# Prompt attention of a two-layer hybrid decoder: the query blocks of a head in the order 0, 7, 1, 6, 2, 5, 3, 4

## The chip, the cores and the metric

The kernel runs on one core of one Trainium2 chip. The metric is the device time of one execution in microseconds. The times are those of whole executions; a profile is of one execution and shows its span from the first to the last instruction.

## What is computed

One inference step of two consecutive layers for a prompt of 1024 tokens and a decode batch of 8 sequences with 4 new tokens each. A layer has an input projection, an mLSTM group of heads and a latent attention (MLA) group of heads, an output projection, a convolutional FFN and a per-layer input embedding. The change lies in the prompt's part of the latent attention, which the reference sweeps in blocks of 128 queries, each against the keys up to its own end:

```python
    def one_block(i):
        q = lax.dynamic_slice_in_dim(qcat, i * qb, qb, axis=1)
        s = jnp.einsum('bqhd,bkd->bhqk', q, lat).astype(jnp.float32) * scale
        qpos = i * qb + jnp.arange(qb)
        s = jnp.where(kpos[None, :] <= qpos[:, None], s, -jnp.inf)
        p = jax.nn.softmax(s, axis=-1).astype(vals.dtype)
        return jnp.einsum('bhqk,bkr->bqhr', p, vals)
    o = lax.map(one_block, jnp.arange(nb))
```

The kernel computes it with keys and values expanded per head, 4 heads of 128 + 64 query columns and 128 value columns, in float32. Block i of a head has i + 1 key tiles of 128, so block 7 is eight times as long as block 0. The blocks don't depend on each other.

## The kernel before, in words

The program loops over the two layers (L2201). In each it projects the input (`mix_projection`), prepares queries, keys and values (`mla_prepare`), runs the prompt's attention (`mla_prompt`, L1356), the decode batch's attention (`mla_sample`, L1485), the output projection, the FFN and the embedding. Each of these is a phase of its own: it ends in a barrier over all engines (L142), so no work of the next phase begins before the last instruction of this one.

`mla_prompt` has a list `blocks` of 32 pairs (head h, query block i), which sets the order of the work on every engine. Each engine's instructions are written out by hand against the place n in this list; buffers go by n modulo 2 (scores: two PSUM banks each; probabilities and their transposes in SBUF: two of each; output: a PSUM bank each), and the groups of up to four transposes go through two PSUM banks by a running number q. Columns of queries, keys and output go by h and i.

- TensorE: scores of block 0; then in step n the scores of block n+1 (L1389 for the 128 plain columns, L1390 for the 64 rotated ones, one pair for each 512 keys), the value products of block n-1 (L1400, one matmul for each key tile), a wait for `p_made` of block n, and its transposes (L1416, one for each key tile). In the trace a float32 matmul of L1389, L1390 or L1400 is two records and a transpose one, so x12 at L1400 is six key tiles.
- VectorE, per block: adds the causal mask (L1453), takes the row maximum (L1458), turns it into the bias of the exponential (L1460); after the exponential the reciprocal of the row sum (L1473) and the scaling of the probabilities (L1475). In step n it does the reciprocal and the scaling of block n, then mask, maximum and bias of block n+1, then the copy of the output of block n-2 (L1466).
- ScalarE: the exponential of block n (L1438), then the copies of the transposes of block n-1 from PSUM (L1429), one for each group of up to four key tiles.
- SyncE issues the loads of 32 pages of the decode batch's cache (L1354), which the next phase reads, and waits for them at the end.

The order inside a step stands here:

```python
            for n in range(len(blocks)):
                if n + 1 < len(blocks):
                    scores(n + 1)
                if n:
                    values(n - 1)
                pe.wait_ge(ph["p_made"], n + 1)
```

`values(n)` waits for `pt_made` up to the last group of block n and for the output bank; `scores(n)` waits for the exponential of block n-2, whose banks it writes.

Of the kernel before, what the change touches and what calls it, by code (L numbers as in the profile page):

```python
# [33 lines left out]
A_HEADS, A_NOPE, A_ROPE, A_DV = 4, 128, 64, 128  # L34
# [1321 lines left out]
def mla_prompt(nc, core, kr, qn, qr, kn, vt, cat, pages):  # L1356


    with ExitStack() as st:
# [6 lines left out]
            exp_done=1, rec_step=1, p_made=1, tr_done=1, pt_made=1, o_done=1, o_used=1, pages_loaded=1))  # L1366
        ps = core.psum
        QT = SEQ // P
        blocks = [(h, i) for h in range(A_HEADS) for i in range(QT)]
        groups = [[(n, j0, min(j0 + 4, i + 1)) for j0 in range(0, i + 1, 4)] for n, (h, i) in enumerate(blocks)]  # L1370
        first_group = np.cumsum([0] + [len(g) for g in groups]).tolist()

# [805 lines left out]
def build_program(nc, operands, n_pool):  # L2178
# [4 lines left out]
    with ExitStack() as whole:  # L2183
# [17 lines left out]
        with nc.Fori(0, DEPTH) as l:  # L2201
            core.l = l
            load_phase(nc, [(core.vec[:], core.vec_in[ds1(l)].rearrange("l p n -> (l p) n"))])
            mem = MixTensors(core.slab)
            mix_projection(nc, core, mem)
            mla_prepare(nc, core, mem)
            pages = [core.slab.at(M_PAGES + i * PW, f"pages_{i}", [P, PW]) for i in range(4)]
            mla_prompt(nc, core, mem.kr, mem.qn, mem.qr, mem.kn, mem.vt, mem.cat, pages)
            mla_sample(nc, core, mem.ckv, mem.kr, mem.qn, mem.qr, mem.cat, pages)
            X = core.slab.at(X_AT, "x", [P, KX, NT])  # L2210
            out_projection(nc, core, mem.cat, X)
            conv_ffn(nc, core, X)
            layer_embedding(nc, core, X)
# [160 lines left out]
```

## Time and profile before

| | us |
|---|---|
| runs, median (lowest to highest) of 3 | 3465.0 (3461.5 to 3472.26) |
| the profiled execution | 3464.91 |
| its span | 3463.1 |
| prompt attention, layer 0 (443.2 to 585.2) | 142.0 |
| prompt attention, layer 1 (2149.8 to 2288.6) | 138.8 |

The mean granted clock of TensorE over the span is 0.944 of full speed. TensorE is busy for 90% of the span, VectorE for 45%, ScalarE for 31% and GpSimd for 4%. In the rows PE is TensorE, DVE is VectorE, ACT is ScalarE. A row of the timeline has the start in us from the span's start, the length in us, the engine, the line of the kernel, the operation, what is written and read, the shapes and how many instructions were merged; in brackets stands how long the engine had been idle before it, and what ended that.

### The profile page before, as it was taken

How to read it: one execution, taken by the hardware profiler on the slowest of the kernel's cores; microseconds unless marked ns; L12 is line 12 of the kernel's file. 1: busy time of each engine (PE TensorE's matmuls, PEld its weight loads, DVE VectorE, ACT ScalarE, POOL GpSimd, SP SyncE). 2: the span in 40 equal slices, each digit the busy share in tenths (PEclk: the TensorE clock that was granted, in tenths of full speed). 3: DMA queues.
4: the chain of work that ended last, by engine and by line, in shares of the span. 5: the costliest groups of instructions: out<-in, count | busy, mean ns of one | idle time of the engine just before them, and what ended most of it. 6: DMA issues, size and time to landing. Idle time of an engine off the chain costs nothing. (4 is left out here: it accounts for less than half of the span.)

```text
span 3463.1 us, 49081 instructions
## 1 busy us (share of the span) xinstructions
PE 3104.8 (90%) x19219; PEld 2881.7 (83%) x19219; DVE 1541.2 (45%) x2460; ACT 1064.0 (31%) x1994; POOL 144.5 (4%) x248
## 2 busy tenths in 40 slices
PE   5998898498999999997979988966899999999887
PEld 5997754298999999997979976535899999999887
DVE  4233543235554445447351354522454445445563
ACT  4232322214223332334242223322233332333241
POOL 0000300000000000000000021000000000000000
PEclk9998899699999999998989989987999999999998
DMA  5102131402111111102131021223111111111023
GB/s 206 47 25 80 45 110 40 167 15 78 49 38 49 37 50 49 50 13 85 42 123 37 19 78 68 83 82 139 41 49 50 37 50 49 39 48 44 10 92 132
DMA packets 58324, 220.52 MB, mean 64 GB/s; under 512 B 6635, under 2 KB 22507, under 8 KB 42995
## 3 DMA queue, kind: packets, MB, share of 16 engines
q1 hardware_dynamic: 58098, 217.27, 17.5%
q8 instruction: 172, 2.82, 0.3%
q14 instruction: 54, 0.43, 0.0%
HBM read 189.72 MB, written 27.52 MB: 63 GB/s over the span
## 5 line engine op out<-in xcount | busy, mean ns | idle before, releaser
L209 PE MATMUL psum<-h_high,conv_ffn_weight_parts 128*128 128x352 f32 x2112 | 689.9, 327 | 21.8 <-DVE h_low L314 14.3
L211 PE MATMUL psum<-h_high,conv_ffn_weight_parts 128*128 128x352 f32 x2112 | 686.3, 325 | 0.0
L210 PE MATMUL psum<-h_low,conv_ffn_weight_parts 128*128 128x352 f32 x2112 | 682.3, 323 | 0.0
L1909 DVE SCALAR_TENSOR_TENSOR conv_sum<-u_padded,vectors,conv_sum 128x1024 f32<-128x1024 f32 x176 | 226.1, 1285 | 594.3 <-ACT conv_sum L1858 581.8
L209 PEld LDWEIGHTS psum<-h_high,conv_ffn_weight_parts 128*128 128x128 f32 x2112 | 400.5, 190 | 24.9 <-issue 23.4
L210 PEld LDWEIGHTS psum<-h_low,conv_ffn_weight_parts 128*128 128x128 f32 x2112 | 399.0, 189 | 0.0
L211 PEld LDWEIGHTS psum<-h_high,conv_ffn_weight_parts 128*128 128x128 f32 x2112 | 396.8, 188 | 0.0
L209 PE MATMUL psum<-g_parts,conv_ffn_weight_parts 128*128 128x352 f32 x1056 | 345.8, 327 | 27.2 <-DVE g_parts L1920 16.3
L211 PE MATMUL psum<-g_parts,conv_ffn_weight_parts 128*128 128x352 f32 x1056 | 343.5, 325 | 0.0
L210 PE MATMUL psum<-g_parts,conv_ffn_weight_parts 128*128 128x352 f32 x1056 | 343.3, 325 | 0.0
L1928 DVE TENSOR_TENSOR x<-x,psum 128x352 f32<-128x352 f32 x528 | 255.5, 517 | 119.4 <-PE psum L211 118.5
L1854 ACT ACTIVATE u_padded<-psum 128x352 f32<-128x352 f32 (+1 forms) x264 | 120.4, 456 | 540.1 <-PE psum L211 540.1
L209 PEld LDWEIGHTS psum<-g_parts,conv_ffn_weight_parts 128*128 128x128 f32 x1056 | 200.3, 190 | 33.5 <-issue 16.8
L209 PE MATMUL psum<-h_high,_projection_weight_parts 128*128 128x352 f32 x576 | 191.9, 333 | 14.3 <-DVE h_low L314 14.3
L210 PEld LDWEIGHTS psum<-g_parts,conv_ffn_weight_parts 128*128 128x128 f32 x1056 | 200.2, 190 | 0.0
L211 PEld LDWEIGHTS psum<-g_parts,conv_ffn_weight_parts 128*128 128x128 f32 x1056 | 199.4, 189 | 0.0
L1867 ACT ACTIVATE g_parts<-conv_sum 128x1056 fp32r<-128x1056 f32 x44 | 47.8, 1087 | 486.9 <-PE psum L211 404.5
L211 PE MATMUL psum<-h_high,_projection_weight_parts 128*128 128x352 f32 x576 | 187.3, 325 | 0.0
L210 PE MATMUL psum<-h_low,_projection_weight_parts 128*128 128x352 f32 x576 | 186.9, 324 | 0.0
L1858 ACT ACTIVATE conv_sum<-psum,vectors 128x352 f32<-128x352 f32 x264 | 170.7, 647 | 0.0
L203 DVE TENSOR_TENSOR conv_ffn_weight_parts<-conv_ffn_weight_stage,conv_ffn_weight_parts 128x2048 fp32r<-128x2048 f32 x66 | 151.1, 2290 | 23.9 <-ACT conv_ffn_weight_parts L197 23.9
L209 PE MATMUL psum<-heads_high,_projection_weight_parts 128*128 128x352 f32 x384 | 126.5, 330 | 23.4 <-DVE heads_low L1706 23.4
(332 smaller groups left out, 5454.3 us busy)
## 6 DMA issues: line engine op xcount, KB each, us to landing
conv_ffn_weight_stage<-w_up_dram SPq DMA_DIRECT2D x44, 1024.0 KB, 5.0
conv_ffn_weight_stage<-w_down_dram SPq DMA_DIRECT2D x22, 1024.0 KB, 4.8
_projection_weight_stage<-w_in_dram SPq DMA_DIRECT2D x18, 1024.0 KB, 4.8
pages<-cache_dram SPq DMA_DIRECT2D x64, 288.0 KB, 4.3
mix_work<-x_residual SPq DMA_DIRECT2D x16, 528.0 KB, 3.8
x<-x_residual SPq DMA_DIRECT2D x2, 4224.0 KB, 16.5
x_residual<-x SPq DMA_DIRECT2D x16, 528.0 KB, 2.7
_projection_weight_stage<-w_out_dram SPq DMA_DIRECT2D x8, 1024.0 KB, 5.9
```

The lines of the kernel that those rows point to most:

```text
L203: dve.tensor_tensor(dst[:, 1, 0:width], self.stage[:, slot % self.stages, 0:width], dst[:, 0, 0:width].bitcast(F32), ALU.subtract).then_in ...
L209: pe.matmul(out, lhs[0], rhs[0], start=first, stop=False)
L210: pe.matmul(out, lhs[0], rhs[1], start=False, stop=False)
L211: return pe.matmul(out, lhs[1], rhs[0], start=False, stop=last)
L1854: act.activation(u[:, q, 2 + c * CH:2 + c * CH + n], src[:, 0:n], ACT.Copy)
L1858: op = act.activation(t[:, q, chunk(c)], src, ACT.Identity, bias=bias, scale=w2)
L1867: act.activation(gp[:, 0, slot, :], t[:, 1, :], ACT.Copy).then_inc(ph["ghi_made"], 1)
L1909: dve.scalar_tensor_tensor(t[:, q, 0:SEQ], row[:, tap:tap + SEQ], w, t[:, q, 0:SEQ], ALU.mult, ALU.add).then_inc(ph["conv_step"], 1)
L1928: dve.tensor_tensor(X[:, k, chunk(c)], X[:, k, chunk(c)], ps[:, (6 + n) % 8, 0:CH], ALU.add).then_inc(ph["x_made"], 1)
```

## The change

The order of the blocks within a head becomes 0, 7, 1, 6, 2, 5, 3, 4 in place of 0 to 7. Nothing else is changed: the list still has the 32 pairs, head by head.

```diff
--- before.py
+++ after.py
@@ -1366,7 +1366,8 @@
             exp_done=1, rec_step=1, p_made=1, tr_done=1, pt_made=1, o_done=1, o_used=1, pages_loaded=1))
         ps = core.psum
         QT = SEQ // P
-        blocks = [(h, i) for h in range(A_HEADS) for i in range(QT)]
+        order = [i for pair in zip(range(QT // 2), range(QT - 1, QT // 2 - 1, -1)) for i in pair]
+        blocks = [(h, i) for h in range(A_HEADS) for i in order]
         groups = [[(n, j0, min(j0 + 4, i + 1)) for j0 in range(0, i + 1, 4)] for n, (h, i) in enumerate(blocks)]
         first_group = np.cumsum([0] + [len(g) for g in groups]).tolist()
```

## Rows read from the trace of the kernel before

**Rows 1.** The page, part 1: busy time, share of the span, instructions.

```profile
PE 3104.8 (90%) x19219; PEld 2881.7 (83%) x19219; DVE 1541.2 (45%) x2460; ACT 1064.0 (31%) x1994; POOL 144.5 (4%) x248
```

**Rows 2.** Stretches: the stage in layers 0 and 1, then two inside it.

```profile
core 0: us, PE busy (x) PEld busy (x) DVE busy (x) ACT busy (x) POOL busy (x), PEclk, DMA share, GB/s
443.20:585.20 142.00, 135.98 (x624) 78.97 (x624) 66.83 (x192) 46.96 (x113) 0.00 (x0) 0.95 0.20 67
2149.80:2288.60 138.80, 132.74 (x624) 77.59 (x624) 66.81 (x192) 46.96 (x113) 0.00 (x0) 0.98 0.21 69
444.70:458.30 13.60, 13.46 (x26) 5.95 (x26) 5.65 (x20) 3.30 (x11) 0.00 (x0) 0.50 0.52 174
2151.40:2158.10 6.70, 6.52 (x13) 2.79 (x13) 3.15 (x13) 2.14 (x8) 0.00 (x0) 0.50 0.34 101
```

**Rows 3.** TensorE's waits, stage of layer 0: us in total, times, longest.

```profile
PE psum L1400 <- ACT probs_T L1429: 5.5, 5, 1.6
```

**Rows 4.** Timeline, layer 0, block 7 of a head, its seam, the next seam.

```profile
508.82 1.60 PE L1400 MATMUL psum<-probs_T,a_v 128*128 128x128 f32 x12
...
510.26 0.93 PE L1416 MATMUL psum<-constants,probs 128*128 128x128 f32 x7
...
511.02 0.39 PE L1389 MATMUL psum<-a_k,a_q_nope 128*128 128x128 f32 x2
...
511.81 0.97 ACT L1429 ACTIVATE probs_T<-psum 128x512 f32<-128x512 f32 x2
...
512.14 0.75 DVE L1475 TENSOR_SCALAR probs<-probs,softmax_rows 128x1024 f32<-128x1024 f32 x1
...
512.83 1.83 PE L1400 MATMUL psum<-probs_T,a_v 128*128 128x128 f32 x14 [1.01 <-ACT probs_T L1429]
...
514.50 1.04 PE L1416 MATMUL psum<-constants,probs 128*128 128x128 f32 x8
...
546.07 1.83 PE L1400 MATMUL psum<-probs_T,a_v 128*128 128x128 f32 x14 [1.01 <-ACT probs_T L1429]
```

**Rows 5.** Timeline, layer 0, the first short blocks of the next head.

```profile
515.37 0.60 PE L1389 MATMUL psum<-a_k,a_q_nope 128*128 128x256 f32 x2
...
516.52 2.05 PE L1400 MATMUL psum<-probs_T,a_v 128*128 128x128 f32 x16
...
518.41 0.27 PE L1416 MATMUL psum<-constants,probs 128*128 128x128 f32 x1
...
518.52 0.81 PE L1389 MATMUL psum<-a_k,a_q_nope 128*128 128x384 f32 x2
518.78 0.28 ACT L1429 ACTIVATE probs_T<-psum 128x128 f32<-128x128 f32 x1 [0.61 <-PE psum L1416]
...
520.10 0.49 PE L1400 MATMUL psum<-probs_T,a_v 128*128 128x128 f32 x2
...
520.43 0.38 PE L1416 MATMUL psum<-constants,probs 128*128 128x128 f32 x2
```

**Rows 6.** Timeline, layer 0, block 4 of that head.

```profile
526.37 0.94 PE L1400 MATMUL psum<-probs_T,a_v 128*128 128x128 f32 x6
...
528.64 0.59 ACT L1429 ACTIVATE probs_T<-psum 128x512 f32<-128x512 f32 x1
...
528.97 0.55 DVE L1475 TENSOR_SCALAR probs<-probs,softmax_rows 128x640 f32<-128x640 f32 x1
```

**Rows 7.** Timeline, layer 0, the end of the stage.

```profile
579.31 1.83 PE L1400 MATMUL psum<-probs_T,a_v 128*128 128x128 f32 x14 [1.65 <-ACT probs_T L1429]
...
580.97 1.04 PE L1416 MATMUL psum<-constants,probs 128*128 128x128 f32 x8
...
582.81 2.05 PE L1400 MATMUL psum<-probs_T,a_v 128*128 128x128 f32 x16 [0.80 <-ACT probs_T L1429]
```

**Rows 8.** Timeline, layer 0, the start of the stage.

```profile
443.28 0.46 PE L1389 MATMUL psum<-a_k,a_q_nope 128*128 128x128 f32 x2 [1.72 <-PEq L142]
...
444.08 0.70 PE L1389 MATMUL psum<-a_k,a_q_nope 128*128 128x256 f32 x2
```

## The prediction

> **What bounds the kernel now.** I read the busy shares first, then the busy time and granted clock of the stretches in which the prompt attention runs, then TensorE's waits there, then its timeline through one head. TensorE is busy for 90% of the span [rows 1]. The change touches one stage, which runs once per layer, for 142.0 and 138.8 us; in it TensorE is busy 96% of the time, VectorE under half, ScalarE a third [rows 2]. So what counts is the time in which TensorE stands still. The waits view finds 5.5 us per layer, all of it in front of the value products, on ScalarE's copies of the transposed probabilities [rows 3].
>
> Call S(i), V(i) and T(i) the scores, value products and transposes of the block with i+1 key tiles. TensorE's order in step n is S of block n+1, V of block n-1, a wait for block n's probabilities, T of block n. While block n goes through mask, maximum, exponential, reciprocal and scaling on VectorE and ScalarE, TensorE has V(n-2), T(n-1), S(n+1) and V(n-1) to do: that is its cover. The timeline gives both. Matmul ends are modelled and overlap, so I take lengths of PE work between starts. V(7) runs 516.52 to 518.41, 1.89 us, and V(0) 520.10 to 520.43, 0.33: 0.11 + 0.222 per key tile. T(7) is 0.87 and T(0) 0.11: 0.109 per tile. S(1) is 1.15 and S(2) 1.58 [rows 4, 5]. S(0) is 0.80, at a point where the clock was still full [rows 8].
>
> The chain of block 7, counted from the end of its scores (V(5) starts at 508.82): the copies behind its exponential start at 511.81, after 2.99 us; the scaling ends at 512.14 + 0.75 = 512.89, and with 0.05 us from the end to TensorE's start (as between the copies' end at 512.78 and V(6) at 512.83) the transposes can go after 4.12 us [rows 4]. The chain of block 4, from 526.37: the copy of the block before it (0.59) ends at 529.23, so V can go after 2.91 us; scaled at 529.52, so T after 3.20 [rows 6]. Blocks 5 and 6 lie between, at about 3.5 and 3.8 (estimates between those two).
>
> As a check, the seam of before: V(6) is ready 4.01 us after the end of S(7), TensorE gets there after V(5) 1.44, T(6) 0.76, S(0) 0.80 = 3.00, so it should wait 1.01 us, and the row has 1.01 [rows 4]. In rising order every other block finds a cover as long as its chain, as the cover grows with it.
>
> **The change, term by term.** It removes and adds no instruction: the S, V and T of a head are the same and sum to the same TensorE time. It only changes who covers whom. No DMA is moved: the 32 page loads of this stage are issued by SyncE without a wait on a block. The terms, per layer:
>
> 1. Removed: the seam 7 to 0 between heads, 3 x 1.01 = 3.03 us. Removed at the end: V(6) without a next S in its cover waits 4.01 - 2.20 = 1.81, and the last T(7) to V(7) takes 1.84 for 0.87 of transposes, 0.97 idle [rows 7]. Sum 5.81. (The waits view shows somewhat less for the last two, since it counts from modelled ends.) The very first T also waits a little for block 0, which I take as 0.14: between 0 and, at most, a short chain of 2 us less S(1), 1.15.
>
> 2. Added, block 7 beside two short ones: cover V(4) 1.22 + T(0) 0.11 + S(1) 1.15 + V(0) 0.33 = 2.81 against 4.12. Wait 1.31 us, in two pieces. V(0) comes first, in TensorE's queue, and its copy stands behind exp(7) on ScalarE: ready at 2.99 + 0.28 + 0.05 = 3.32, reached at 2.48, so 0.84; then T(7) 0.47 more. Queued behind these waits is all of TensorE's work, so they are on the path. 3 heads x 1.31 = 3.93.
>
> 3. Added, the same in the first head, which has no V(4) before it: 4.12 - 1.59 = 2.53.
>
> 4. Added, block 4 beside 3 and the next head's 0: V(3) is reached at V(5) 1.44 + T(3) 0.44 + S(0) 0.80 = 2.68 and ready at 2.91: 0.23, three times 0.69.
>
> 5. The end on block 4: V(3) is reached at 1.88, ready at 2.91: 1.03. The last T(4) to V(4) saves 0.31 of the second copy (0.28 for 0.59): 1.84 - 0.31 - 0.55 = 0.98. Sum 2.01.
>
> 6. At nothing: block 6 (cover V(7) 1.89 + T(1) 0.22 + S(2) 1.58 + V(1) 0.55 = 4.24 against 3.8), block 5 (V(6), T(2), V(2) and more than S(2): over 4.3 against 3.5), blocks 1, 2, 3 and the next 0, whose chains start when VectorE is free of the long one and are over under the following long scores (7, 6, 5 and 8 tiles of keys, where S(2) with 3 takes 1.58). If that cover went, a short chain of about 2 us would show. The leads of 0.4 us for block 6 are the thinnest.
>
> Per layer 9.16 - 5.95 = +3.2 us, so +6.4 for two; the head's period goes from 33.24 (V(6) at 512.83 to V(6) at 546.07 [rows 4]) to 33.8.
>
> 7. The clock at the start. The granted clock stands at half, the 1.2 GHz level, for 13.6 us in layer 0 from 444.7 on and for 6.7 us in layer 1 [rows 2], while TensorE works nearly all the time, so half of each is lost: 3.35 us in layer 1, and 3.2 more in layer 0, by which the two stages differ. In the new order S(7) comes second; it is about 4.1 us of work (an estimate: 0.43 more per tile than S(2) up to four tiles, 2.01, and twice that). At half clock it fills those first 7 us, so layer 1 loses the same 3.35. In layer 0 S(7) would end at about 451.7 (3.5 us of it done at half clock), block 7's chain runs to 455.8, where a slow TensorE costs nothing because it waits anyway (its cover of 1.59 takes 3.2), and only the 2.5 us to 458.3 cost again: 3.5 + 1.25 = 4.8 lost in place of 6.55, a gain of 1.7. So +6.4 - 1.7 = +4.7. Bounds on this term: -3.2 (layer 0 needs no second stretch at half clock and nothing comes instead) to +6.4 (the 2.53 us of idleness in the first head brings one more stretch in each layer, each 3.2).
>
> The profiled execution took 3464.9 us for a span of 3463.1, 0.1 from the median of 3465.0. Forecast: 3464.9 + 4.7 = 3469.6 us, +0.14%. A measurement of this kernel can tell about 0.3%, 10.4 us, from no change, so this is no change, with a lean to the slow side.
>
> **Rivals.** (a) Slower, by the clock: every seam now has 1.31 us of waits in two pieces within 2 us, and TensorE's clock goes to half behind each. For it: at the start of the stage the clock fell after a pause of 1.7 us in front of S(0) [rows 2, 8]. Against: it stayed full across the 1.01 us seams, and across 1.81 and 0.97 us near the end of the stage, for the granted clock of the whole stage is 0.95 and 0.98, which the two stretches at its start account for alone (6.8 of 142.0, 3.35 of 138.8) [rows 2, 7]. Price: 3.2 us for each fall, at 8 seams 25.6, 3495 us. It decides from two falls on (4.7 + 6.4 = 11.1 against the bound of 10.4). Chance 0.17.
> The Trainium skill, TensorE: Matmul & The Clock Gate, "A second HAM failure mode: psum-queue depth-cycling", says that short idle times between groups of matmuls that cycle through PSUM banks can make the clock swing between its levels. By that rule this change comes out at rival (a); the trace so far speaks against it.
>
> (b) Faster, the pairing works as a cover: if V(0) did not have to stand behind exp(7) and the long chain were covered, terms 2 to 4 vanish and 3464.9 - 2 x (5.95 - 2.01) = 3457.0. For it: per pair, cover and chain balance in sum. Against: the queues are in order and the cover of block 7 is counted from rows. Chance 0.03 (and 0.02 for the clock's best bound with a good measurement).
>
> (c) The change doing nothing: the expression gives 0, 7, 1, 6, 2, 5, 3, 4, and all buffers go by the place n, all columns by i, so the order does change. That leaves 3465 only as a sum that cancels, inside the forecast's case.
>
> **How the numbers follow.** Forecast's case 0.78, within 0.3%: 3465 to 3476 by the bounds of term 7 and 0.15 us of error in each of some ten waits. Rival (a) with a few falls only reaches 3480. Range 3464 to 3479. Same 0.78; slower 0.17; faster 0.05.
>
> **What would show it.** In the waits view, idle time in front of V on ScalarE's copies rises from 5.5 us per layer to about 7, and T shows waits on VectorE's scaling that it hardly has now, about 0.47 each at four places, 1.9; together near 9. From one head's block 7 mask to the next 33.8 us. The stage in layer 1 takes 142 us. The step on the clock is wrong if a stretch at half clock stands anywhere but at the stage's start; the whole reading is wrong if the waits on block 7 are absent, or if S, V or T change in length.

## The result and the profile after

The changed kernel takes 3476.9 us (median of 20 runs, 3469.2 to 3485.8) against 3469.8 (20 runs, 3461.5 to 3483.7) for the kernel before. The ratio is 1.0018 with a 95% interval of 1.0010 to 1.0025: 6.2 us slower, 3.5 to 8.7 (the two medians lie 7.1 us apart). That is inside the 0.3% that the prediction called no change, and on its slow side; a ratio of 1 lies outside the interval. The forecast was 3469.6, +4.7 us. Its base, 3464.9, came from three runs; over 20 runs the kernel before takes 4.9 us more than that, so the measured 3476.9 stands 7.3 us above the forecast, most of it by the base, and it is the difference that tests the working.

The busy time and granted clock of the stage in both layers of the changed kernel, the answer to [rows 2]; the last number but two is the granted clock:

```profile
core 0: us, PE busy (x) PEld busy (x) DVE busy (x) ACT busy (x) POOL busy (x), PEclk, DMA share, GB/s
444.10:587.60 143.50, 136.65 (x624) 78.72 (x624) 66.53 (x192) 46.71 (x113) 0.00 (x0) 0.95 0.20 67
2150.80:2294.30 143.50, 136.64 (x624) 78.71 (x624) 66.54 (x192) 46.70 (x113) 0.00 (x0) 0.95 0.20 67
445.80:459.30 13.50, 12.64 (x24) 5.20 (x23) 4.38 (x13) 3.48 (x9) 0.00 (x0) 0.50 0.52 176
2152.50:2166.00 13.50, 12.64 (x24) 5.20 (x23) 4.38 (x13) 3.48 (x9) 0.00 (x0) 0.50 0.55 176
```

The stage takes 143.5 us in either layer, where it took 142.0 and 138.8: +1.5 and +4.7. Layer 1 now has the same 13.6 us at half clock as layer 0. (The windows in these rows lie just inside the stretch; read to its ends it is 13.65 us, written 13.6 or 13.7 here, and the short one is 6.8.) The span is 3467.4 us, 4.3 longer: 6.2 from the two stages, and 2 us less elsewhere, where nothing was changed.

TensorE's waits in the stage of layer 0 (us in total, times, longest), the answer to [rows 3]. Line numbers are one higher than before:

```profile
PE psum L1401 <- ACT probs_T L1430: 5.5, 9, 0.9
...
PE psum L1417 <- DVE probs L1476: 1.0, 3, 0.3
```

The same 5.5 us on ScalarE's copies, in nine waits in place of five, and 1.0 us on VectorE's scaling that was not there. The seam at block 7, from the timeline of layer 0, the answer to [rows 4]; the last row is V(4) one head later:

```profile
487.50 1.38 PE L1401 MATMUL psum<-probs_T,a_v 128*128 128x128 f32 x10
...
488.72 0.27 PE L1417 MATMUL psum<-constants,probs 128*128 128x128 f32 x1
488.83 0.60 PE L1390 MATMUL psum<-a_k,a_q_nope 128*128 128x256 f32 x2
...
490.49 0.27 ACT L1430 ACTIVATE probs_T<-psum 128x128 f32<-128x128 f32 x1
...
490.81 0.49 PE L1401 MATMUL psum<-probs_T,a_v 128*128 128x128 f32 x2 [0.76 <-ACT probs_T L1430]
490.83 0.75 DVE L1476 TENSOR_SCALAR probs<-probs,softmax_rows 128x1024 f32<-128x1024 f32 x1
...
491.63 1.09 PE L1417 MATMUL psum<-constants,probs 128*128 128x128 f32 x8 [0.33 <-DVE probs L1476]
...
492.56 1.02 PE L1390 MATMUL psum<-a_k,a_q_nope 128*128 128x512 f32 x2
...
521.35 1.38 PE L1401 MATMUL psum<-probs_T,a_v 128*128 128x128 f32 x10
```

From the end of S(7), 487.50: V(0) starts after 3.31 us, behind its copy, which stands behind the long exponential; T(7) after 4.13. Forecast were 3.32 and 4.12. A head takes 521.35 - 487.50 = 33.85 us; 33.8 was forecast, 33.24 it was.

### The profile page after: what moved, and what is told of

It reads as the page before. It is cut to its first block and busy times, and to the rows that moved or that the text cites. A ratio compares the mean times of both kernels' runs of the same rounds, so it can differ in the third digit from the quotient of the medians.

```text
span 3467.4 us, 49081 instructions
## 1 busy us (share of the span) xinstructions
PE 3111.6 (90%) x19219; PEld 2884.7 (83%) x19219; DVE 1541.2 (44%) x2460; ACT 1063.6 (31%) x1994; POOL 144.5 (4%) x248
## 5 line engine op out<-in xcount | busy, mean ns | idle before, releaser
L209 PEld LDWEIGHTS psum<-g_parts,conv_ffn_weight_parts 128*128 128x128 f32 x1056 | 199.8, 189 | 33.6 <-issue 16.8
L203 DVE TENSOR_TENSOR conv_ffn_weight_parts<-conv_ffn_weight_stage,conv_ffn_weight_parts 128x2048 fp32r<-128x2048 f32 x66 | 151.2, 2290 | 23.9 <-ACT conv_ffn_weight_parts L197 23.9
```

The lines of the kernel that those rows point to most:

```text
L203: dve.tensor_tensor(dst[:, 1, 0:width], self.stage[:, slot % self.stages, 0:width], dst[:, 0, 0:width].bitcast(F32), ALU.subtract).then_in ...
L209: pe.matmul(out, lhs[0], rhs[0], start=first, stop=False)
```

## Experiments

In all of them the result is set against runs of the kernel before on the same chip. The stage's time is read from the profile; the stretch at half clock at its start is read from its ends (granted clock 0.50) and can be checked by the stage's mean clock: 0.97 or 0.98 is 6.8 us, 0.96 is 10.2, 0.95 is 13.6, 0.94 is 17.1, as long as the clock is full from there to the end of the stage.

### Neighbours of like length

```diff
-        order = [i for pair in zip(range(QT // 2), range(QT - 1, QT // 2 - 1, -1)) for i in pair]
+        order = [0, 2, 4, 6, 7, 5, 3, 1]
```

> Order 0, 2, 4, 6, 7, 5, 3, 1 in every head: each block stands between neighbours of nearly its own length, also across the heads. My theory (the cover of a block's softmax chain is V of two blocks before, T of the block before, S of the next, V of the block before, all counted from rows): block 7 has V(4) 1.22 + T(6) 0.76 + S(5) 3.26 + V(6) 1.66 = 6.9 us of cover against 4.12, and no block of a head waits; what is left is about 0.8 us at the end of the stage. TensorE's waits fall from 5.5 us per layer to about 1, a head takes 32.25 us (33.24 before, 33.85 after the change), and the time falls by 5.1 us per layer, 10 us in all: ratio 0.997 to the kernel before. Rival (mixing lengths costs in itself, since TensorE's order and the two buffers are made for neighbours that grow by one): waits of 0.2 to 1 us stay at the steps of two, ratio 1.000 or above.

Ratio 0.9984 (0.9975 to 0.9992), 3465.6 us against 3472.5. The waits of the stage in layer 0:

```profile
PE psum L1390 <- PEq L142: 1.7, 1, 1.7
PE psum L1401 <- ACT probs_T L1430: 1.3, 2, 0.7
```

and the row of T(7) of its first head in the timeline:

```profile
465.63 0.75 DVE L1476 TENSOR_SCALAR probs<-probs,softmax_rows 128x1024 f32<-128x1024 f32 x1
...
467.55 1.83 PE L1401 MATMUL psum<-probs_T,a_v 128*128 128x128 f32 x14
469.21 1.04 PE L1417 MATMUL psum<-constants,probs 128*128 128x128 f32 x8
```

The scaling of block 7 ends at 466.38, TensorE asks for it at 469.21. (The first row of the waits is the barrier at the stage's start, alike in all kernels.) A head takes 32.34 us, 32.25 and the 0.11 us at V(3). So the covers counted from rows hold, and mixing lengths costs nothing where the cover is there. At the end of the stage 1.3 us were left, where I expected 0.8. The stage takes 136.3 us in both layers, 10.2 of them at half clock at the start. That is 7.2 us less per layer than the changed order. In the whole time I expected 10 us, and 5.6 were measured (2.8 to 8.7): by the two stages it is 8.2 against the profile of before shown above and 5.3 against the second one below.

### The mirror image

```diff
-        order = [i for pair in zip(range(QT // 2), range(QT - 1, QT // 2 - 1, -1)) for i in pair]
+        order = [1, 3, 5, 7, 6, 4, 2, 0]
```

> Order 1, 3, 5, 7, 6, 4, 2, 0 in every head, the mirror image of the pyramid. Theory (covers from rows): the 0.11 us that the pyramid waits at V(3), whose cover had only S(0), goes, since the block with S(0) as its next one, 2, has V(6) 1.66 + T(4) 0.55 + S(0) 0.81 = 3.02 us before V(4), ready at 2.7. No wait inside the stage but at its end, about 0.8 us; a head takes 32.25 us. Stage 136.0 us, less whatever the clock at the start does; ratio to before 0.998. Rival: the steps of two leave their own waits, 0.1 to 0.3 us per head as in the pyramid.

Ratio 0.9980 (0.9969 to 0.9992). A wait of 0.17 us stood before V(4) in every head, so the 2.7 us that I gave for its copies were too short, and a head took 32.40 us, not 32.25. The rival was right in this. The stages:

```profile
446.20:584.30 138.10, 136.06 (x624) 78.66 (x624) 67.16 (x192) 47.60 (x113) 0.00 (x0) 0.95 0.21 69
2153.00:2288.00 135.00, 132.88 (x624) 77.12 (x624) 67.18 (x192) 47.61 (x113) 0.00 (x0) 0.97 0.22 71
```

138.1 us in layer 0 and 135.0 in layer 1, with 13.7 and 6.8 us at half clock: the same program, 3.1 us apart by one more stretch, as in the kernel before.

### The pairs read backwards

```diff
-        order = [i for pair in zip(range(QT // 2), range(QT - 1, QT // 2 - 1, -1)) for i in pair]
+        order = [3, 4, 2, 5, 1, 6, 0, 7]
```

> Order 3, 4, 2, 5, 1, 6, 0, 7, the changed order read backwards, so the same pairs. Theory: what counts are the four pieces of cover, not who is whose partner. Block 7 now has V(6) 1.66 + T(0) 0.11 + S(3) 2.01 + V(0) 0.33 = 4.11 against 4.12, so no wait; block 6 has V(5) 1.44 + T(1) 0.22 + S(0) 0.81 + V(1) 0.55 = 3.02 against 3.83, so 0.8 us; block 5 has V(2) ready at 3.05 and reached at 2.70, so 0.35 us. A head takes 33.4 us (33.85 in the changed kernel). At the end of the stage 3.0 us. Rival (block 7 beside block 0 is the cost): waits of 1.3 us stay at block 7 and a head takes 33.85 us.

One execution, 3483.1 us. Waits of 0.28 us at V(2) and 0.72 at V(1) in each head (0.81 in the first; 0.35 and 0.8 were expected), none at block 7 except behind the last one; a head takes 33.53 us. So block 7 beside block 0 costs nothing with S(3) and V(6) around it: the pairing is not the cost, the four pieces of cover are. The stage's waits in layer 0:

```profile
PE psum L1401 <- ACT probs_T L1430: 6.2, 10, 1.4
...
PE psum L1417 <- DVE probs L1476: 0.3, 1, 0.3
```

The stage is nonetheless long, 146.1 and 145.7 us. At its end block 7 has only V(6) and T(0) as cover, and TensorE waits three times within 4.1 us; the end in layer 0, and the granted clock of two stretches there:

```profile
584.70 0.49 PE L1401 MATMUL psum<-probs_T,a_v 128*128 128x128 f32 x2 [1.37 <-ACT probs_T L1430]
585.52 1.09 PE L1417 MATMUL psum<-constants,probs 128*128 128x128 f32 x8 [0.33 <-DVE probs L1476]
587.41 3.78 PE L1401 MATMUL psum<-probs_T,a_v 128*128 128x128 f32 x16 [0.80 <-ACT probs_T L1430]
...
583.00:586.70 3.70, 1.91 (x13) 1.25 (x12) 1.73 (x7) 1.80 (x4) 0.00 (x0) 1.00 0.00 0
586.80:591.50 4.70, 3.78 (x16) 3.49 (x16) 0.26 (x1) 0.56 (x2) 0.00 (x0) 0.50 0.00 0
```

The clock fell to half at 586.7, inside the third of these waits, 4.8 us before the stage ended, and V(7) took 3.78 us in place of 2.05. In layer 1 it was the same, 4.4 us before the end. No other kernel showed that.

### ScalarE's copy ahead of the long exponential

```diff
+                early = n > 0 and blocks[n - 1][1] == 0
+                if early:
+                    transposed(n - 1)
                 act.activation(pr[:, b, 0:(i + 1) * P],
...
-                if n:
+                if n and not early:
                     transposed(n - 1)
```

> The changed order, but ScalarE copies the transposes of block 0 before the exponential of block 7, not behind it. My theory (the length of block 7's chain against its cover of 2.81 us sets the seam, and the copy's place only splits the wait): V(0) no longer waits, T(7) waits the whole 1.3 us, a head still takes 33.85 us, the time is that of the changed kernel, ratio 1.0018 to before. Rival (the copy that stands behind the long exponential is the cost): the 0.84 us at three seams and the 2.06 us in the first head go, 4.6 us per layer, ratio 0.9992 to before.

The seam of this kernel in the timeline of layer 0:

```profile
491.48 1.38 PE L1401 MATMUL psum<-probs_T,a_v 128*128 128x128 f32 x10
...
493.96 0.49 PE L1401 MATMUL psum<-probs_T,a_v 128*128 128x128 f32 x2
...
495.78 1.09 PE L1417 MATMUL psum<-constants,probs 128*128 128x128 f32 x8 [1.33 <-DVE probs L1479]
```

V(0) waits no more, and T(7) waits it all: it starts 4.30 us after S(7)'s end, 0.17 later than before, because the copy now holds up the exponential by as much. A head takes 34.01 us. So the copy's place splits the wait and doesn't make it; moving it costs a little. The time, though, went up more than that: ratio 1.0035 (1.0022 to 1.0048). The profile shows where:

```profile
448.00:591.80 143.80, 136.28 (x624) 78.70 (x624) 66.25 (x192) 46.64 (x113) 0.00 (x0) 0.95 0.20 67
2155.00:2305.20 150.20, 142.73 (x624) 82.00 (x624) 66.25 (x191) 46.88 (x113) 0.00 (x0) 0.91 0.19 64
2156.30:2180.10 23.80, 22.70 (x48) 10.36 (x47) 7.23 (x20) 4.58 (x11) 0.00 (x0) 0.50 0.64 207
2275.90:2279.10 3.20, 3.20 (x10) 1.76 (x8) 1.21 (x5) 1.65 (x4) 0.00 (x0) 0.50 0.02 5
```

In layer 1 the start stood at half clock for 23.8 us, and the clock fell once more, at 2275.8, 0.1 us after the wait of 1.33 us at the last head's T(7), for 3.4 us. That makes the two stages together 7.0 us longer than in the changed kernel, about what the ratio shows (1.0035 against 1.0018 is 5.9 us). All five executions took 3481.7 to 3486.8 us, but only this one has a profile. I took a second one:

> The kernel with block 0's copy ahead of the exponential of block 7 once more, for a second profile. Theory (one wait of 1.33 us in place of 0.84 and 0.49 is what the clock does not bear): again stretches at half clock behind some seam inside the stage, or a start of over 20 us at half clock, in at least one layer. Rival (chance): 13.6 us at the start in both layers and full clock from there, stages of 143.8 us.

This one took 3475.8 us and showed neither: 13.7 us at the start in both layers, full clock from there, stages of 143.8 us. So with one wait of 1.33 us the clock can fall at a seam, and it did at one of the 12 seams that were reached at full clock in two profiles. In the changed kernel, with 0.84 and 0.49 us (by starts), it fell at none of 12. One fall doesn't show that the joining of the waits is the cause, and why the first ratio was 1.0035 stays open beyond its one profile.

### The changed kernel again, and the kernel before again

> The changed kernel once more, for a second profile. Theory (the second stretch at half clock comes with block 7 standing second in the first head): 13.6 us at half clock at the start of the stage in both layers, stages of 143.5 us. Rival (chance): about 7 us in one or both, that stage 1.5 to 3 us shorter.

> The kernel before once more, for a second profile. A stage of 142.0 us where the start shows 13.6 us at half clock, of 138.8 us where it shows 6.8. If the rising order brings the shorter stretch in at least one of the two layers again, as in three of four so far, the first head's order has to do with it; if both show 13.6, the difference between the orders was chance.

The changed kernel: 143.5 and 143.6 us, 13.7 us at half clock in both layers. The kernel before:

```profile
444.40:583.40 139.00, 132.55 (x624) 77.43 (x624) 66.80 (x192) 46.95 (x113) 0.00 (x0) 0.98 0.21 69
2154.60:2293.50 138.90, 132.61 (x624) 77.44 (x624) 66.76 (x192) 46.97 (x113) 0.00 (x0) 0.98 0.21 69
446.50:453.10 6.60, 6.03 (x12) 2.46 (x11) 3.35 (x12) 1.87 (x8) 0.00 (x0) 0.50 0.39 115
2156.50:2163.10 6.60, 6.15 (x13) 2.47 (x11) 3.17 (x12) 2.08 (x8) 0.00 (x0) 0.50 0.40 113
```

6.8 us in both. The 13.6 us of layer 0 in [rows 2] was the rarer case of the kernel before, not what layer 0 is like.

### Only the first head, or only the others

```diff
-        blocks = [(h, i) for h in range(A_HEADS) for i in order]
+        blocks = [(h, i) for h in range(A_HEADS) for i in (order if h else range(QT))]
```

> The first head of each layer rises from 0 to 7, the other three go in the changed order. My theory by waits: 1.0 us at the seam 7 to 0, 0.64 us at the first block 7 that has V(7) in its cover, 1.31 at two seams, 0.23 at two, 2.0 at the end, 6.9 us per layer with the start, 0.9 above the kernel before: ratio 1.0005. On the clock, theory: the pause of 2.5 us in the first head brings the second stretch at half clock, so here at least one of the two layers shows only about 7 us at half clock at the start of the stage. Rival: that second stretch is chance, and both layers may show 13.6 us here too.

Ratio 1.0001 (0.9990 to 1.0012). Its stages:

```profile
448.40:588.30 139.90, 133.57 (x624) 77.60 (x624) 66.49 (x192) 46.55 (x113) 0.00 (x0) 0.98 0.21 68
2158.30:2298.30 140.00, 133.50 (x624) 77.53 (x624) 66.48 (x192) 46.57 (x113) 0.00 (x0) 0.98 0.21 68
```

6.8 us at half clock in both. The waits are as counted: 1.01 at the seam, 0.42 in two pieces at the first block 7 in the waits view, 0.76 + 0.33 at the later ones.

```diff
-        blocks = [(h, i) for h in range(A_HEADS) for i in order]
+        blocks = [(h, i) for h in range(A_HEADS) for i in (range(QT) if h else order)]
```

> Only the first head of each layer goes in the changed order, the other three rise. My theory by waits: 2.5 us in the first head, 0.2 at its end, 1.0 at each of the two seams 7 to 0, 2.8 at the end: 7.6 us per layer, 1.6 above the kernel before, 3.2 in all; with the second stretch at half clock in both layers some 1.5 to 3 us more: ratio 1.001 to 1.0018. Both layers show 13.6 us at half clock at the start of the stage. Rival (the three steady heads make the loss): ratio 1.0003 or less, and the stretch at half clock is 7 us in one of them as before.

Ratio 1.0013 (1.0004 to 1.0022). Its stages:

```profile
446.30:588.00 141.70, 135.77 (x624) 78.64 (x624) 66.83 (x192) 46.98 (x113) 0.00 (x0) 0.95 0.21 67
2156.90:2298.60 141.70, 135.76 (x624) 78.61 (x624) 66.83 (x192) 46.95 (x113) 0.00 (x0) 0.95 0.21 67
```

13.6 us at half clock in both. The changed order lost 4.6 us per layer against the usual 138.9 of the kernel before: its first head alone loses 2.8 (141.7), its other three heads alone 1.1 (139.9 and 140.0). The parts add up to 3.9 of 4.6; the seams that each of the two kernels has between the orders differ from both pure ones, and I did not take that apart.

### Block 7 second, but covered

```diff
-        order = [i for pair in zip(range(QT // 2), range(QT - 1, QT // 2 - 1, -1)) for i in pair]
+        order = [0, 7, 6, 5, 4, 3, 2, 1]
```

> Order 0, 7, 6, 5, 4, 3, 2, 1 in every head. Block 7 stands second as in the changed kernel, but its cover has S(6): in a later head V(1) 0.55 + T(0) 0.11 + S(6) 3.69 + V(0) 0.33 = 4.68 us against 4.12, in the first head 4.13. Theory on the waits: none inside a head, 32.3 us per head, waits only at the end of the stage. On the clock, theory A (the pause at block 7 of the first head brings the second stretch): here the stretch at the stage's start is 7 to 10 us in at least one layer. Theory B (it comes with the long scores that stand second, pause or not): 13.6 us in both layers, stages of about 138 us. Ratio to before 0.997 by A, 0.999 by B.

Ratio 0.9988 (0.9973 to 1.0003). No wait inside a head, 32.23 us each, and the stage still takes 139.2 us:

```profile
443.20:582.40 139.20, 137.65 (x624) 79.08 (x624) 66.93 (x192) 47.99 (x113) 0.00 (x0) 0.94 0.21 69
2149.80:2289.00 139.20, 137.65 (x624) 79.09 (x624) 66.90 (x192) 48.00 (x113) 0.00 (x0) 0.94 0.21 69
444.70:461.50 16.80, 16.80 (x28) 6.21 (x27) 4.84 (x12) 2.69 (x6) 0.00 (x0) 0.50 0.58 195
2151.30:2168.20 16.90, 16.90 (x28) 6.24 (x27) 4.85 (x12) 2.81 (x7) 0.00 (x0) 0.50 0.58 189
```

TensorE works without a pause for 16.8 us, and all of them at half clock. (The whole stretch at half clock is 17.1 us.) So theory A, that the pause at block 7 brings the second stretch, fell. Theory B, that it comes with the long scores that stand second, fits, but its numbers were too small: 13.6 us and a stage of about 138 us, against 17.1 and 139.2. That the long scores are the cause is not shown, and why is open. By first head, the stretch at half clock at the start of the stage was, over all profiles:

| order of the first head | kernels | us at half clock, layer 0 / layer 1 |
|---|---|---|
| 0, 1, 2, 3 ... | before, twice; first head rising; the last one below | 13.7/6.8, 6.8/6.8, 6.8/6.8, 6.8/13.7 |
| 0, 2, 4, 6 ... | pyramid | 10.2/10.2 |
| 1, 3, 5, 7 ... | its mirror | 13.7/6.8 |
| 3, 4, 2, 5 ... | pairs backwards | 13.7/13.7 |
| 0, 7, 1, 6 ... | changed, twice; first head paired; copy ahead, twice | 13.7/13.7 three times, 13.7/23.9, 13.7/13.7 |
| 0, 7, 6, 5 ... | this one | 17.1/17.1 |

Part of the scatter goes with the moment at which the clock fell, read from the granted clock in windows of 0.05 us. In the eight layers whose first head rises it fell 1.26 to 1.92 us after the first matmul of the stage: in the two that then stood at half clock for 13.7 us after 1.26 and 1.43, in the six with 6.8 us after 1.51 to 1.92. With 0, 7, 1, 6 ... it fell after 1.29 to 1.88 us in ten layers, eight of them between 1.51 and 1.92, and none had less than 13.7. So the moment of the fall doesn't explain the difference between these two orders.

### A version from what was learned

```diff
-        order = [i for pair in zip(range(QT // 2), range(QT - 1, QT // 2 - 1, -1)) for i in pair]
-        blocks = [(h, i) for h in range(A_HEADS) for i in order]
+        valley = [6, 4, 2, 0, 1, 3, 5, 7]
+        blocks = [(h, i) for h in range(A_HEADS)
+                  for i in (range(QT), valley, valley, range(QT - 1, -1, -1))[h]]
```

> First head 0 to 7, second and third 6, 4, 2, 0, 1, 3, 5, 7, last head 7 to 0. Theory on the waits: every seam has long beside long, so no wait over 0.2 us inside the stage, and about 1.2 us at its end on block 0. Theory on the clock: the first head is the one of the kernel before, so the stretch at half clock at the stage's start is 6.8 us as in five of six such layers so far. Together a stage of 134.5 to 135 us in both layers (138.8 before at the same clock, 143.5 in the changed kernel, 136.3 in the pyramid), ratio to before 0.9975. Rival on the clock: the start is a matter of chance, a stretch of 10 to 14 us in one or both layers, stages of 136 to 138 us, ratio 0.998 to 0.999.

```profile
444.70:579.50 134.80, 132.55 (x624) 77.45 (x624) 67.01 (x192) 47.41 (x113) 0.00 (x0) 0.97 0.22 71
2155.50:2293.20 137.70, 136.00 (x624) 78.96 (x624) 67.10 (x192) 47.39 (x113) 0.00 (x0) 0.95 0.21 69
```

134.8 us where the start was short, the shortest stage of all, and 137.7 where it was 13.7 us. So the theory on the clock held in one layer of two, and the ratio, 0.9985 (0.9974 to 0.9997), is the rival's and not the 0.9975 that I expected. Of the waits inside the stage that the order makes, none is over 0.17 us; T(0) at its start waited 0.58 us in layer 0, as in the second profile of the kernel before (0.57), and the end 0.53 and 0.43. By these ratios to the kernel before it beats both kernels, and so do the pyramid (0.9984) and its mirror (0.9980); between the three the intervals don't decide.

## Why the prediction was right, and where not

**The bound.** Right: TensorE's standing still is what the order changes. S, V and T kept their lengths (V(4) 1.22 and T(0) 0.11 by starts, the record of V(0) 0.49 in both), but for T(7), up from 0.87 to 0.93 where it starts after a wait.

**Terms 1 to 5, the waits.** Terms 2, 4 and 5 are right to 0.1 us each, and so are the seams and the end of term 1. Its 0.14 us for the very first T was 0 and 0.2 in the first profile of the kernel before and 0.6 and 0.5 in the second, inside the bounds that I gave. The head went from 33.24 to 33.85 (33.8 forecast). The wait at V(0) was 0.84 by starts as forecast; at T(7) 0.49 (0.47); at V(3) 0.23 (0.23). The term that was short is T(7) itself after a wait, 0.06 us more, in each of three heads. In the waits view I expected about 9 us per layer and 6.5 stood there. 1.7 of that was my slip: I added term 3, the first head's 2.53 us, at full clock, though term 7 has that head at half clock, where its cover is twice as long, and the view shows 0.84 there. The rest is how the view counts, from modelled ends (0.76 + 0.33 at a seam for 1.33 by starts), which I had said of term 1 and not applied. The chain itself was right there too: T(7) of the first head starts 4.14 us after the end of its scores (452.12 to 456.26 in layer 0), where I had 4.12.

**Term 6, at nothing.** Right: no wait at blocks 1, 2, 5 and 6, and at 3 none but the one of term 4.

**Term 7, the clock at the start.** This is the step that failed, in its size. For layer 0, at an equal stretch of 13.6 us, I forecast +3.2 - 1.7 = +1.5 and the stage gave 143.5 - 142.0 = +1.5. For layer 1 I wrote that it would lose the same 3.35 as before, +3.2, a stage of 142 us; it gave +4.7 and 143.5 us, since it now has 13.6 us at half clock in place of 6.7. My own terms give that 4.7 once the stretch is in them: +3.2 by the waits, +3.2 for the further stretch, -1.7 for the part of it in which TensorE waits anyway. I took the stretch of each layer in one profile for a property of that layer. With the second profile the kernel before has 6.8 us in three of four layers, the changed one 13.7 in four of four. The upper bound of the term had one more stretch in it, but for the reason of the pause, and the run with block 7 covered showed that the pause is not needed.

**The sum.** 4.7 forecast, 6.2 measured (3.5 to 8.7). That 4.7 lies in this interval is partly luck: I booked a gain of 1.7 for the long stretch of layer 0, which was the rarer case, and nothing for layer 1, where a stretch was added. Against the kernel before with its usual short stretches the changed one loses 9.2 us by the stages, twice 4.6. My text also ended its range for no change at 3476, though 6.4 us by the waits and the upper bound of term 7 make 3477.7. By stages, two profiles each: before 142.0, 138.8, 139.0, 138.9, after 143.5 three times and 143.6, so twice 3.9 = 7.7 us, within that interval. The rest of the program took 3180 to 3200 us in the profiles of kernels whose code there is the same, so a single profile says little on 5 us of the whole, and the stage must be read alone.

**Rival (a)**, a fall of the clock at every seam: not seen at any of the 12 seams at full clock in two profiles of the changed kernel, the stage's mean of 0.95 being the start's alone. The rule of the Trainium skill (TensorE: Matmul & The Clock Gate, "A second HAM failure mode: psum-queue depth-cycling") that went with it, that short idle times between groups of matmuls can make the clock swing, did not come about in this kernel. The rival was nearer than my text made it, though: with the two waits joined, one fall was seen. It lasted 3.4 us, so my price of 3.2 us for each fall, taken from a stretch of 6.8, was about twice too high for it.

**Rival (b)**, the pairing as a cover: not so; it is the neighbours on both sides that cover, and the orders that put long beside long gained what the pairing did not.

## What to carry to other kernels

In a software pipeline written out by hand, write down for each step the chain that must be hidden and the pieces of work that lie over it, here V of two before, T of one before, S of the next, V of one before, and order the work so that the longest chain has its longest neighbours around it. Balancing long against short does the opposite: it takes cover from the chain that needs it and gives it to one that doesn't. Where the clock changes during a stage, take its stretches from several profiles before a term is built on one.

## What the runs showed of the hardware

- At the start of this stage TensorE stood at half clock for 6.8 to 23.9 us while it was nearly always busy; in one kernel it worked 16.8 us without a pause and the clock stayed at half until then. The length of it went with the order of the first blocks and, where the first head rose, with the moment of the fall (table above and the lines under it); the cause is open. Each further 6.8 us cost 2.9 to 3.2 us of the stage (137.7 against 134.8, 138.1 against 135.0, 142.0 against 138.8).
- The clock bore waits of 0.8 and 0.5 us with 0.3 us of work between them at 12 seams, and waits of 1.0 us at all 12 seams of the kernel before. It fell after one of 12 waits of 1.33 us, and near the end of a stage, in two of two layers of one profile, in the third of three waits (1.4, 0.3 and 0.8 us) within 4.1 us. It did not fall before the end of the stage in the kernel before, where the waits of 1.65 and 0.80 us ended 3.5 us apart.
- A group of eight transposes took 0.06 us longer by starts behind a wait (0.93 in the changed kernel against 0.87 before).
